# Scaling the exponentials by the reciprocal sums before they are turned, in the second block's attentions, in place of turned reciprocals

## The chip, the cores and the metric

The kernel runs on one NeuronCore of one Trainium2 chip. The metric is the device time of one execution in microseconds (us): 3101.95 us, the median of 3 runs (3101.36 to 3105.1). TensorE (PE in the profile) multiplies and turns tiles; VectorE (DVE), ScalarE (ACT) and GpSimd (POOL) do the elementwise work; SyncE (SP) issues the DMAs. Each engine runs its own list of instructions in order, and semaphores tie the lists together.

## The reference, cut to what matters

Two transformer blocks in float32 on 1024 tokens of width 1024. The first block is not touched. The second has two layers, and each has a memory attention (4 heads of 64, 256 keys); the first layer also has a causal attention of 12 heads. What both compute:

```python
def causal_attention(q, k, v):            # 12 heads; q, k of 96 features, v of 64
    ...                                   # in query blocks of 128 rows
    sc = einsum('bqhd,bkhd->bhqk', q_blk, k) * scale
    sc = where(mask, sc, -inf)
    p = softmax(sc, axis=-1)
    out = einsum('bhqk,bkhd->bqhd', p, v)

def memory_attention_2(q, mem_k, mem_v):  # 4 heads of 64, 256 keys, no mask
    p = softmax(einsum('bshd,bmhd->bhsm', q, mem_k) / sqrt(64), axis=-1)
    return einsum('bhsm,bmhd->bshd', p, mem_v)
...
y = concatenate([tok, mem_out], axis=-1) * silu(gate)
h = layer_norm(ALPHA * h + y @ w_out, ln_g, ln_b)
```

A softmax row is exp(score - maximum) divided by its sum. The division may be done at the end, on the attention's output, or before the product with v, on the exponentials.

## The kernel before, in words

The program is first written as one list, `work`, of records (`emit(kind, r)`); each engine then goes through the whole list and issues its part of every record, with the waits that the record names. So the order in which the Python code emits records is the order on every engine, and nothing is reordered later.

An attention is cut into *units*: one head and one block of 128 queries. Two heads make a *pair*, a first unit (s = 0) and a second one (s = 1, with `mate` set to the first). A unit of the causal attention with query block qt has nblk = qt + 1 key blocks of 128, so its exponentials E are 128 x 128 nblk; a memory unit has nblk = 2. There are 32 memory units in each of the two layers and 96 causal units: 16 + 16 + 48 = 80 pairs. The causal units come as six columns of 16 units (p = 0 to 5), each with nblk = 8, 8, 7, 7, ... 1, 1.

The life of a unit:
- `scores`: TensorE computes the scores in pieces of up to 512 keys; VectorE copies each piece from PSUM into E, scaled (and masked), with the row minimum (L3233, L3238). A causal unit with over 4 blocks has two pieces and a small reduction of the two minima (L3243).
- `exp`: ScalarE takes the exponential of the whole of E in place and sums its rows into `den` (L2998).
- `combine`: for the second unit of a pair, `r_spread`. VectorE waits for both exponentials, takes the reciprocals of the two sums (L3247, 128 x 2) and copies each over 64 columns of a 128 x 128 tile O (L3251).
- `probs`: TensorE turns E in blocks of 128 x 128, up to four into one PSUM place (L2898); ScalarE (L3004) and VectorE (L3269) in turn copy the place into PT.
- `pair_values`: TensorE multiplies PT with v for both heads (L2921), which gives the output with features on the partitions. There the reciprocals are needed along the free axis, so TensorE also turns O (L2924).
- `pair_mul`: VectorE multiplies the gate by the turned reciprocals (L3384) and then by the output (L3386).

`Att.steps` sets the order. Step i emits, in a round: the values of the unit i - 4 if it is the second of its pair (at the start of the step), then in turns a piece of the scores of unit i, a turn of unit i - 2, and the `combine` of unit i - 1; then `pair_mul` and one piece of `fill`, other work of TensorE: gate strips beside the first memory units, projections of the next causal heads beside the causal ones. In the causal attention the exp of unit i comes after its last piece, so on VectorE the order of a step is: first piece of unit i, combine of unit i - 1, second piece of unit i, copy of turned blocks of unit i - 2, reduction. The memory attentions (`together=True`) score the two units of a pair in one even step. E has three buffers in the causal attention (mE), four in the others (gE, nE, lE with one from `cols`); the scores have two PSUM places.

The causal attention lies between 2405 and 2686 us of the span, the memory attention of the first layer at 2282 to 2405 us, that of the second layer at 2830 to 2997 us beside the recurrent branch. There are fewer fills than steps in the causal attention: none runs beside the last 26 units or so, nor beside the last and first few units where column 1 and column 3 begin.

## Time and profile before

| | |
|---|---|
| median of 3 runs | 3101.95 us |
| the profiled execution's own time | 3105.86 us |
| its span | 3104.1 us |
| TensorE busy | 3032.0 us (98%) |
| VectorE busy | 1915.0 us (62%) |
| ScalarE busy | 1373.9 us (44%) |
| GpSimd busy | 717.3 us (23%) |
| TensorE's granted clock over the span | 0.995 of full speed |

The span goes from the first to the last instruction of the profiled execution; the rest of its time lies around it. A busy TensorE is not one at its peak: the end of a matmul is modelled, so the start of one to the start of the next tells what it costs the engine. Idle time of an engine is put down to what came last. A mean over a stage hides that steps of 1 block and of 8 blocks have different limits.

### The profile page before, as it was taken

How to read it: one execution, taken by the hardware profiler on the slowest of the kernel's cores; microseconds unless marked ns; L12 is line 12 of the kernel's file. 1: busy time of each engine (PE TensorE's matmuls, PEld its weight loads, DVE VectorE, ACT ScalarE, POOL GpSimd, SP SyncE). 2: the span in 40 equal slices, each digit the busy share in tenths (PEclk: the TensorE clock that was granted, in tenths of full speed). 3: DMA queues.
4: the chain of work that ended last, by engine and by line, in shares of the span. 5: the costliest groups of instructions: out<-in, count | busy, mean ns of one | idle time of the engine just before them, and what ended most of it. 6: DMA issues, size and time to landing. Idle time of an engine off the chain costs nothing.

```text
span 3104.1 us, 50426 instructions
## 1 busy us (share of the span) xinstructions
PE 3032.0 (98%) x18252; PEld 2572.1 (83%) x18252; DVE 1915.0 (62%) x3747; ACT 1373.9 (44%) x2723; POOL 717.3 (23%) x926
## 2 busy tenths in 40 slices
PE   7999999999999999999999999999999999999999
PEld 7988888999999788888788888888977777687677
DVE  6657675263543655675888887876353657753675
ACT  5446565444444444332333333455433556522552
POOL 3424334366643000001111111001101111022230
PEclk9999999999999999999999999999999999999999
DMA  5110011122211333652233225644100000221012
GB/s 200 43 37 30 21 35 50 31 66 72 72 56 35 138 127 102 227 189 90 72 107 109 106 102 191 210 150 141 51 29 22 16 28 29 96 82 58 28 62 102
DMA packets 96808, 264.84 MB, mean 85 GB/s; under 512 B 19568, under 2 KB 24176, under 8 KB 84144
## 3 DMA queue, kind: packets, MB, share of 16 engines
q1 hardware_dynamic: 96560, 261.61, 24.4%
q8 instruction: 146, 2.39, 0.3%
q14 instruction: 102, 0.84, 0.1%
HBM read 200.69 MB, written 60.62 MB: 84 GB/s over the span
## 4 chain that ended last, share of the span: by engine, by line
PE 85%; DVE 6%; ACT 3%; POOL 2%; issue 2%; DMA 1%; SPq 0%; DVEq 0%; POOLq 0%; ACTq 0%
PE ps L2847 66%; PE ps L2890 7%; PE ps L2898 3%; PE ps L2854 2%; PE ps L2905 2%; PE ps L2921 2%; PE ps L2913 1%; POOL gs L3451 1%; PE ps L2924 1%; PE ps L2941 1%; POOL stats L3459 1%; POOL wlo L3447 1%; DVE qk L3224 0%; DVE hlo L3193 0%; DVE wlo L3116 0%
## 5 line engine op out<-in xcount | busy, mean ns | idle before, releaser
L2847 PE MATMUL ps<-whi,hhi 128*128 128x256 f32 (+2 forms) x1920 | 579.4, 302 | 2.6 <-DVE hlo L3193 1.3
L2847 PE MATMUL ps<-whi,hlo 128*128 128x256 f32 (+2 forms) x1920 | 562.7, 293 | 0.0
L2847 PE MATMUL ps<-wlo,hhi 128*128 128x256 f32 (+2 forms) x1920 | 561.8, 293 | 0.0
L2847 PEld LDWEIGHTS ps<-whi,hhi 128*128 128x128 f32 x1920 | 368.1, 192 | 12.5 <-issue 4.4
L2847 PEld LDWEIGHTS ps<-wlo,hhi 128*128 128x128 f32 x1920 | 368.6, 192 | 7.6 <-issue 0.2
L2847 PEld LDWEIGHTS ps<-whi,hlo 128*128 128x128 f32 x1920 | 368.1, 192 | 7.6
L3456 POOL TENSOR_SCALAR stats<-stats 128x2 f32<-128x2 f32 (+2 forms) x230 | 58.5, 254 | 1142.7 <-ACT xsf L2955 490.0
L3445 POOL CAST whi<-raw 128x512 fp32r<-128x512 f32 (+2 forms) x180 | 113.6, 631 | 832.8 <-PE ps L2847 805.5
L2847 PE MATMUL ps<-hhi,whi 128*128 128x512 f32 x640 | 255.6, 399 | 0.2 <-DVE hlo L3116 0.2
L2847 PE MATMUL ps<-hhi,wlo 128*128 128x512 f32 x640 | 249.9, 390 | 0.0
L2847 PE MATMUL ps<-hlo,whi 128*128 128x512 f32 x640 | 249.2, 389 | 0.0
L3447 POOL TENSOR_TENSOR wlo<-raw,whi 128x512 fp32r<-128x512 f32 (+2 forms) x180 | 230.1, 1278 | 14.4
L3459 POOL TENSOR_TENSOR stats<-stats 128x2 f32<-128x2 f32 (+2 forms) x230 | 167.1, 726 | 19.2
L3451 POOL TENSOR_TENSOR fo<-fo,fo 128x512 f32<-128x512 f32 x44 | 71.3, 1620 | 363.4 <-DVE fo L3346 360.8
L2847 PEld LDWEIGHTS ps<-hhi,wlo 128*128 128x128 f32 x640 | 120.1, 188 | 26.1
L2847 PEld LDWEIGHTS ps<-hhi,whi 128*128 128x128 f32 x640 | 120.4, 188 | 23.8 <-issue 1.3
L2847 PEld LDWEIGHTS ps<-hlo,whi 128*128 128x128 f32 x640 | 120.4, 188 | 23.2
L3224 DVE TENSOR_TENSOR qk<-qk,stats 128x256 f32<-128x256 f32 x148 | 97.6, 660 | 48.8 <-POOL stats L3459 44.9
L3214 DVE COPY qk<-ps 128x256 f32<-128x256 f32 x148 | 62.8, 424 | 94.7 <-PE ps L2847 90.0
L2890 PE MATMUL ps<-mkT,mqT 96*128 96x512 f32 (+3 forms) x288 | 117.6, 493 | 2.1 <-DVE mE L3233 1.6
L3238 DVE CUSTOM_DVE_ANT_1 aE<-ps,atab 128x512 f32<-128x512 f32 x128 | 88.5, 692 | 44.6 <-PE ps L2890 41.2
L2998 ACT ACTIVATE mE<-mE,stats 128x1024 f32<-128x1024 f32 (+7 forms) x96 | 74.5, 776 | 92.6 <-DVE stats L3243 64.1
(783 smaller groups left out, 7443.0 us busy)
## 6 DMA issues: line engine op xcount, KB each, us to landing
raw<-in_W SPq DMA_DIRECT2D x60, 1024.0 KB, 4.9
scratch_fs<-fo SPq DMA_DIRECT2D x77, 256.0 KB, 2.0
scr<-scratch_gates SPq DMA_DIRECT2D x48, 256.0 KB, 3.1
scratch_gates<-go SPq DMA_DIRECT2D x46, 256.0 KB, 2.5
wd<-in_WD SPq DMA_DIRECT2D x44, 256.0 KB, 3.5
wf0b<-in_WF SPq DMA_DIRECT2D x10, 1024.0 KB, 5.1
wf1b<-in_WF SPq DMA_DIRECT2D x10, 1024.0 KB, 5.2
scratch_x<-x SPq DMA_DIRECT2D x16, 512.0 KB, 3.1
```

The costliest lines, as they stand in the source:

```text
L2847: x = e.matmul(r.out, a, b, start=(r.start and m == 0), stop=(r.stop and m == n - 1), skip_group_check=r.joined)
L2854: x = e.transpose(place.ps[0:rows, j * 128:(j + 1) * 128], b, ident[:, :])
L2890: x = e.matmul(p.place.ps[:, o:o + n], *p.blocks[b], start=True, stop=True)
L2898: x = e.transpose(r.place.ps[0:n, j * 128:(j + 1) * 128], r.u.E[:, o:o + n], ident[:, :])
L2998: e.activation(r.e, r.e, ACT.Exp, bias=r.nm, scale=-1.0, accum_out=r.den).then_inc(w.sig(r.done), 1)
L3214: e.tensor_copy(r.nb, r.place.ps[:, 0:256]).then_inc(w.sig(r.place.read), 1)
L3224: e.tensor_tensor(n3, n3, bc, ALU.mult).then_inc(w.sig(r.scaled), 1)
L3238: x = e.tensor_tensor_reduce(out=out, in0=src, in1=p.bias, scale=-u.scale, scalar=3e38, op0=ALU.add, op1=ALU.min, accum_out=p.mx)
L3445: e.tensor_copy(r.hi, r.raw).then_inc(w.inner(), 1)
L3447: e.tensor_tensor(r.lo, r.raw, r.hi.bitcast(F), ALU.subtract).then_inc(w.sig(r.lo_done), 1)
L3451: e.tensor_tensor(r.out, r.a, r.b, r.op).then_inc(w.sig(r.done), 1)
L3459: e.tensor_tensor(r.ss, r.ss, half_neg[:, 0:n], ALU.pow).then_inc(w.sig(r.rstd), 1)
```

## The change

`combine` now emits a record `e_norm` for every unit, not `r_spread` for every pair. VectorE takes the reciprocal of the unit's own sum (128 x 1), and E is multiplied by it in place, before it is turned: by VectorE (`tensor_scalar`), or, for the first unit of each pair of the causal attention (`act_norms=True`), by ScalarE (`Copy` with a scale). The tile O, its copy, its turn on TensorE and the first of the two multiplications of the gate are gone. `probs` waits for the scaled E.

```diff
@@ scored
-                    elif not self.paired:
+                    else:
                         x_.den = stat(1)
-                    elif u.mate:
-                        x_.den = u.mate.den2[:, 1:2]
-                    else:
-                        u.den2 = stat(2)
-                        x_.den = u.den2[:, 0:1]
@@ combine
-                if self.paired and u.mate:
-                    u.oi, u.o, u.O_free = self.O.take()
-                    u.spread = signal("r_spread")
-                    emit("r_spread", u)
+                if self.paired:
+                    u.norm_by_act = self.act_norms and not u.mate
+                    u.inverse = signal("e_norm")
+                    u.normed = signal("exp") if u.norm_by_act else u.inverse
+                    u.ecols = u.E[:, 0:128 * u.nblk]
+                    emit("e_norm", u)
+                    u.e_ready = [u.normed]
@@ attM
-        attM = Att(..., [x[:, :] for x in mO], SB2, OB2, paired=True)
+        attM = Att(..., [], SB2, OB2, paired=True, act_norms=True)
@@ TensorE, pair_value
-                    w.wait_ge(*r.spread)
-                    e.transpose(r.v_place.ps[:, 128:256], r.o, ident[:, :]).then_inc(r.v_place.full[0], 1)
+                    x.then_inc(r.v_place.full[0], 1)
@@ ScalarE
+                elif kind == "e_norm" and r.norm_by_act:
+                    w.wait_ge(*w.last)
+                    w.wait_ge(*r.inverse)
+                    e.activation(r.ecols, r.ecols, ACT.Copy, scale=r.dens[0]).then_inc(w.sig(r.normed), 1)
@@ VectorE
-                elif kind == "r_spread":
-                    w.wait_each(r.mate.exps)
-                    w.wait_each(r.exps)
-                    inner(lambda: e.reciprocal(r.mate.den2, r.mate.den2))
-                    w.wait_ge(*w.last)
-                    w.wait_each(r.O_free)
-                    both = r.mate.den2.rearrange("p (s o) -> p s o", o=1).broadcast_to((128, 2, 64))
-                    e.tensor_copy(r.o.rearrange("p (s d) -> p s d", s=2), both).then_inc(w.sig(r.spread), 1)
+                elif kind == "e_norm":
+                    w.wait_each(r.exps)
+                    w.wait_ge(*w.last)
+                    if r.norm_by_act:
+                        e.reciprocal(r.dens[0], r.dens[0]).then_inc(w.sig(r.inverse), 1)
+                    else:
+                        inner(lambda: e.reciprocal(r.dens[0], r.dens[0]))
+                        w.wait_ge(*w.last)
+                        e.tensor_scalar(r.ecols, r.ecols, r.dens[0], None, ALU.mult).then_inc(w.sig(r.normed), 1)
@@ VectorE, pair_mul
-                    inner(lambda: e.tensor_tensor(r.gate, r.v_place.ps[:, 128:256], r.gate, ALU.mult))
-                    w.wait_ge(*w.last)
                     e.tensor_tensor(r.gate, r.v_place.ps[:, 0:128], r.gate, ALU.mult).then_inc(w.sig(r.v_place.read), 1)
```

On VectorE, the two steps that begin with the first piece of the 7-block units of the last causal column, before. mE is E, mPT is PT, `ISA` is the masked copy of a piece (L3238), gT the gate.

```order
L3233 TENSOR_SCALAR mE_393,stats<-ps 128x512
L3247 RECIPROCAL stats<-stats 128x2
L3251 COPY mO_416<-stats 128x128
L3238 ISA mE_393,stats<-ps,tabM 128x384
L3238 ISA stats 128x1
L3269 COPY mPT_414<-ps 128x512
L3243 TENSOR_REDUCE stats<-stats 128x1
L3233 TENSOR_SCALAR mE_394,stats<-ps 128x512
L3384 TENSOR_TENSOR gT<-ps,gT 128x128
L3386 TENSOR_TENSOR gT<-ps,gT 128x128
L3238 ISA mE_394,stats<-ps,tabM 128x384
```

The same steps on VectorE now (the names of the buffers count otherwise).

```order
L3230 TENSOR_SCALAR mE_394,stats<-ps 128x512
L3247 RECIPROCAL stats<-stats 128x1
L3249 TENSOR_SCALAR mE_393<-mE_393,stats 128x1024
L3235 ISA mE_394,stats<-ps,tabM 128x384
L3235 ISA stats 128x1
L3267 COPY mPT_413<-ps 128x512
L3240 TENSOR_REDUCE stats<-stats 128x1
L3230 TENSOR_SCALAR mE_395,stats<-ps 128x512
L3245 RECIPROCAL stats<-stats 128x1
L3382 TENSOR_TENSOR gT<-ps,gT 128x128
L3235 ISA mE_395,stats<-ps,tabM 128x384
```

In the first of the two steps the copy of 128 x 128 has become a scaling of 128 x 1024; in the second a reciprocal, which waits for the exp of the unit before, stands where the first multiplication of the gate was.

On ScalarE in the same place, before and then now: exponentials (L2998, now L2991), copies of turned blocks (L3004, now L3001), and the new scalings (L2995).

```order
L2998 ACTIVATE mE_393,stats<-mE_393,stats 128x1024
L3004 ACTIVATE mPT_415<-ps 128x512
L2998 ACTIVATE mE_394,stats<-mE_394,stats 128x896
L3004 ACTIVATE mPT_413<-ps 128x512
L2998 ACTIVATE mE_395,stats<-mE_395,stats 128x896
```

```order
L2991 ACTIVATE mE_393,stats<-mE_393,stats 128x1024
L3001 ACTIVATE mPT_413<-ps 128x512
L2991 ACTIVATE mE_394,stats<-mE_394,stats 128x896
L3001 ACTIVATE mPT_411<-ps 128x512
L2995 ACTIVATE mE_394<-mE_394,stats 128x896
L2991 ACTIVATE mE_395,stats<-mE_395,stats 128x896
```

The scaling of a first unit stands between the copy of turned blocks of the unit before it and the exp of its second unit.

## Rows read from the trace of the kernel before

**Rows 1.** The page, busy time, share of the span and instructions of each engine
```profile
PE 3032.0 (98%) x18252; PEld 2572.1 (83%) x18252; DVE 1915.0 (62%) x3747; ACT 1373.9 (44%) x2723; POOL 717.3 (23%) x926
```
**Rows 2.** Busy time by stretch: causal attention; second layer's memory attention
```profile
core 0: us, PE busy (x) PEld busy (x) DVE busy (x) ACT busy (x) POOL busy (x), PEclk, DMA share, GB/s
2405.00:2686.00 281.00, 273.89 (x2016) 200.47 (x2015) 188.56 (x632) 162.32 (x340) 34.38 (x48) 0.99 0.06 21
2830.00:2997.00 167.00, 167.00 (x824) 120.65 (x824) 114.35 (x224) 81.01 (x145) 39.00 (x41) 1.00 0.11 39
```
**Rows 3.** Groups of instructions by line: busy us, mean ns, idle before
```profile
L3386 DVE TENSOR_TENSOR gT<-ps,gT 128x128 f32<-128x128 f32 x80 | 23.3, 291 | 2.7
L3247 DVE RECIPROCAL stats<-stats 128x2 f32<-128x2 f32 x80 | 13.3, 167 | 16.9 <-ACT mE L2998 8.5
L3251 DVE COPY mO<-stats 128x128 f32<-128x128 f32 x52 | 12.7, 244 | 2.0 <-DVE stats L3247 0.2
L2924 PE MATMUL ps<-ident,mO 128*128 128x128 f32 x52 | 17.1, 329 | 0.0
```
**Rows 4.** Timeline of TensorE, causal attention: start us, duration us, instruction
```profile
2657.94 0.61 PE L2921 MATMUL ps<-mPT,mV 128*64 128x128 f32 x8
2658.48 0.33 PE L2924 MATMUL ps<-ident,mO 128*128 128x128 f32 x1
2658.65 1.02 PE L2890 MATMUL ps<-mkT,mqT 96*128 96x512 f32 x2
...
2658.48 0.14 PEld L2924 LDWEIGHTS ps<-ident,mO 128*128 128x128 f32 x1 [0.17 <-issue]
```
**Rows 5.** Timeline of TensorE, first memory attention
```profile
2291.86 0.33 PE L2924 MATMUL ps<-ident,gO 128*128 128x128 f32 x1
2292.03 0.38 PE L2898 MATMUL ps<-ident,gE 128*128 128x128 f32 x2
```
**Rows 6.** VectorE by tile or line: durations of scalings, reciprocals of size and scalar operands
```profile
L3140 DVE TENSOR_SCALAR rt<-rt x2: 227/228/228, 2176.8 to 2178.8; 128x128 f32<-128x128 f32 x2
L3414 DVE TENSOR_SCALAR xc<-up,cols x12: 546/547/993, 2829.2 to 2996.5; 128x512 f32<-128x512 f32 x12
L3206 DVE TENSOR_SCALAR stats<-cols x4: 154/154/156, 87.0 to 87.6; 128x1 f32<-128x1 f32 x4
L3396 DVE TENSOR_SCALAR stats<-stats x16: 213/214/215, 2713.3 to 3097.2; 128x1 f32<-128x1 f32 x16
L3262 DVE SCALAR_TENSOR_TENSOR aE<-aE,stats 128x1024 f32<-128x1024 f32 x32 | 45.0, 1408 | 1.1
```
**Rows 7.** Timeline of ScalarE, last causal column: exponentials of units 81 to 84
```profile
2650.05 1.15 ACT L2998 ACTIVATE mE<-mE,stats 128x1024 f32<-128x1024 f32 x1 [1.48 <-DVE stats L3243]
2653.41 1.04 ACT L2998 ACTIVATE mE<-mE,stats 128x896 f32<-128x896 f32 x1 [1.49 <-DVE stats L3243]
2656.31 1.04 ACT L2998 ACTIVATE mE<-mE,stats 128x896 f32<-128x896 f32 x1 [1.13 <-DVE stats L3243]
2659.31 0.94 ACT L2998 ACTIVATE mE<-mE,stats 128x768 f32<-128x768 f32 x1 [1.23 <-DVE stats L3243]
```
**Rows 8.** Waits of VectorE in the causal attention: us in total, times, longest
```profile
DVE mE L3238 <- PE ps L2890: 47.6, 33, 3.1
...
DVE stats L3247 <- ACT mE L2998: 8.5, 17, 0.7
```
**Rows 9.** Timeline where causal column 1 begins: units 16 and 17
```profile
2461.65 1.15 ACT L2998 ACTIVATE mE<-mE,stats 128x1024 f32<-128x1024 f32 x1 [2.30 <-DVE stats L3243]
...
2463.39 0.60 PE L2898 MATMUL ps<-ident,mE 128*128 128x128 f32 x4
...
2464.37 1.15 ACT L2998 ACTIVATE mE<-mE,stats 128x1024 f32<-128x1024 f32 x1 [1.48 <-DVE stats L3243]
```
**Rows 10.** Timeline at the end of the causal attention: unit 94
```profile
2680.53 0.40 ACT L2998 ACTIVATE mE<-mE,stats 128x128 f32<-128x128 f32 x1 [0.56 <-DVE stats L3238]
...
2681.14 0.14 PEld L2898 LDWEIGHTS ps<-ident,mE 128*128 128x128 f32 x1 [0.20 <-issue]
```
**Rows 11.** Copies of spread reciprocals, second memory attention: ns min/median/max
```profile
L3251 DVE COPY lO<-stats x16: 226/227/1290, 2843.0 to 2979.2; 128x128 f32<-128x128 f32 x16
```

More of the change, by code:

```diff
@@ L654, in build, with __init__ @@
         class Att:
-            def __init__(self, E, PT, os_, sb, ob, dve_turns=True, together=False, paired=False, by_feature=False, between=False):
-                self.by_feature, self.between = by_feature, between
+            def __init__(self, E, PT, os_, sb, ob, dve_turns=True, together=False, paired=False, by_feature=False, between=False, act_norms=False):
+                self.by_feature, self.between, self.act_norms = by_feature, between, act_norms
                 self.E, self.PT, self.O, self.sb, self.ob = Slots(E), Slots(PT), Slots(os_), sb, ob
@@ L764, in pair_values @@
                     self.PT.free[x.pi] = [u.v_place.full]
-                self.O.free[u.oi] = [u.v_place.full]
             def values(self, u):
@@ L2405, in build @@
         gPT = [rest(f"gPT{i}", [256], F, (20 + i) * KB) for i in range(3)]
-        gO = [rest(f"gO{i}", [128], F, 23 * KB + 512 * i) for i in range(2)]
         nE = [inh(f"nE{i}", [256], F, (46 + i) * KB) for i in range(4)]
@@ L2409, in build @@
         mPT = [inh(f"mPT{i}", [T], F, (54 + 4 * i) * KB) for i in range(2)] + [rest("mPT2", [T], F, 80 * KB)]
-        mO = [inh(f"mO{i}", [128], F, 62 * KB + 512 * i) for i in range(2)]
         def post_pair(self, u):
@@ L2438, in build @@
         mem_us = mem_units(kv[0], kv_tok[0], qm_tok)
-        attG = Att([x[:, :] for x in gE], [x[:, :] for x in gPT], [x[:, :] for x in gO], SB2, OB2, together=True, paired=True)
+        attG = Att([x[:, :] for x in gE], [x[:, :] for x in gPT], [], SB2, OB2, together=True, paired=True)
         for s_ in (attG.E, attG.PT, attG.O):
@@ L2447, in build @@
         h_free = [m]
-        attN = Att([x[:, :] for x in nE], [x[:, :] for x in nPT], [x[:, :] for x in mO], SB2, OB2, together=True, paired=True)
+        attN = Att([x[:, :] for x in nE], [x[:, :] for x in nPT], [], SB2, OB2, together=True, paired=True)
         for s_ in (attN.E, attN.PT, attN.O):
@@ L2539, in build @@
         n_done[:] = [mem_us[-1].v_full, mem_us[-1].fin, mem_us[-1].s_full]
-        attM = Att([x[:, :] for x in mE], [x[:, :] for x in mPT], [x[:, :] for x in mO], SB2, OB2, paired=True)
+        attM = Att([x[:, :] for x in mE], [x[:, :] for x in mPT], [], SB2, OB2, paired=True, act_norms=True)
         for s_ in (attM.E, attM.PT, attM.O):
@@ L2696, in build @@
         lPT = [rest(f"lPT{i}", [256], F, o * KB) for i, o in enumerate((71, 87))]
-        lO = [rest(f"lO{i}", [128], F, o) for i, o in enumerate((70 * KB + 512, 88 * KB + 256))]
         attL = Att([x[:, :] for x in lE] + [col("q_norm", 0, 256)], [x[:, :] for x in lPT] + [col("lam"), col("q_norm", 256, 256)],
-                   [x[:, :] for x in lO], SB2, DB_FOUR, together=True, paired=True)
+                   [], SB2, DB_FOUR, together=True, paired=True)
         for s_ in (attL.E, attL.PT, attL.O):
```

## The prediction

> **What bounds the kernel now.** I read the page's busy shares first: TensorE 98% of the span, VectorE 62%, ScalarE 44% [rows 1]. So time is what TensorE spends plus what it waits, and the changed stages have to be looked at one by one. The busy time by stretch shows two sorts. In the second layer's memory attention TensorE is busy for all of its 167 us and VectorE for 114: TensorE alone bounds it. The causal attention has TensorE at 274 of 281 us, VectorE at 189, ScalarE at 162 [rows 2]. There the mean hides something, since the end of a matmul is modelled. VectorE idles 47.6 us before L3238 because scores are late, so mostly TensorE is the late one, but 17 of its reciprocals wait for an exp [rows 8]. The timeline of the exponentials in the last causal column shows the other limit: starts at 2650.05, 2653.41, 2656.31 and 2659.31, each of them ended by a VectorE reduction [rows 7]. That is a loop and not TensorE: exp of unit i - 1, then on VectorE the reciprocal that waits for it, the second piece of unit i, the copy of turned blocks, the reduction, and the exp of unit i. I call a step even or odd by its unit i. Before, only even steps hold the wait for the exp (the reciprocals of a pair are taken once), and they take 3.36 us (81 to 82) where the odd one takes 2.90 us (82 to 83).
>
> **The change part by part.** *TensorE loses 80 turns of O.* In the causal attention the turn starts 0.17 us after a pause that stands ahead of it, and the scores start 0.17 us after the turn [rows 4]. The start-to-start cost is therefore 0.34 us at most, if the pause goes too (it stands ahead of the change from values to a turn, and scores follow now). It is 0.11 us at least, which is the step from one turn to the next (four turns span 0.60 us, two 0.38: 0.22 us for two more) [rows 5, 9]. The pause probably goes and the scores' own weight load, 0.18 us of the 0.36 for two, stays partly in sight; I take 0.25. In the memory attentions turns of E follow instead, 0.17 us later [rows 5]; the pause passes to them, and they take over the slower first turn, so I take 0.12, between 0.11 and 0.17. Gain: 32 pairs x 0.12 = 3.8 us; and 48 causal pairs, of which I leave out the 8 of the last column (bound by the loop), 40 x 0.25 = 10.0 us. Sum 13.8 us, bounds 7.9 (72 x 0.11) and 21.8 (48 x 0.34 + 32 x 0.17).
>
> *VectorE's load.* It loses 80 multiplications of 0.291 us, 80 copies of 0.244 and 80 reciprocals of 0.167 [rows 3], and gains 160 reciprocals, which I price at the same 0.167, as a fixed part makes nearly all of it, and 112 scalings: 64 of 128x256, 48 of 128x128 to 128x1024. The trace has no in-place scaling with one per-row scalar. Bounds: 128 wide without such a scalar 0.228 us, 512 wide with two of them 0.546; the scalar costs 0.06 (0.214 against 0.154 for one column) [rows 6]. So 512 wide without is 0.426, the slope 0.516 ns a column, and with one scalar 0.35 us for 256, 0.68 for 896, 0.75 for 1024. The dear side is the in-place two-input form, 1.41 us for 1024 [rows 6]. I take the cheap side, since its rows are the same operation. In the causal attention that is -33.7 us and +16 + 48 x 0.52 = +41 us: VectorE goes from 189 to some 196 of 281 us, no bound by itself. In the memory attentions the sum is 32 x 0.535 less and 32 x 0.167 + 64 x 0.35 more, +10.6 us, hidden behind TensorE, which is busy throughout [rows 2]; were that cover gone, it would cost those 10.6 us.
>
> The Trainium skill (VectorE: DVE Perf Modes, "The perf-mode tier table") gives `tensor_scalar` on float32 in SBUF two elements a cycle and two-input forms one. Rows 6 agree: 0.516 ns a column is half of the 1.04 ns that a cycle takes at the page's 0.96 GHz. By the two-input rate the sum would be the slower rival's.
>
> *ScalarE's load.* 48 copies with a per-row scale, priced as the exp of the same width, 1.15 us for 1024 down to 0.40 for 128 [rows 7, 10], mean 0.78: +37 us, 162 to 199 of 281. Not a bound, but it stands in the way, below.
>
> *The wait that the change adds.* VectorE now waits in every step for the exp of unit i - 1. Queued behind that waiting reciprocal are the second piece of unit i, the copy of turned blocks that frees TensorE's place, and the reduction on which the exp of unit i waits. Even steps keep their wait, but the 0.23 us copy becomes a scaling of the 8- or 7-block unit: 0.75 - 0.23 = +0.52 us. Odd steps get the loop. I price it from the even step measured: 3.36 us, less 0.11 for the shorter exp (1.04 for 1.15), plus 0.06 for one multiplication of the gate instead of the copy, 3.31 against 2.90: +0.41. A pair of 7-block units takes 0.93 us more. This shows only where the loop and not TensorE sets the pace. Columns 1, 3 and 5 have no fill there, and columns 2 and 4 are about balanced, column 0 half: 5.5 x 0.93 = 5.1 us. The odd step of the 8-block pair in columns 1, 3 and 5, 2.72 us from exp to exp [rows 9], gets about the same 0.4: 1.2 us. In column 5 the 6- and 5-block pairs lose perhaps 0.3 and 0.2: 0.5 us. In columns 2 and 4 a fill's copy, the copy of turned blocks and the scaling queue up on ScalarE in an odd step: 0.3 each, 0.6 us.
>
> *Latency of a first unit.* Its turns need exp, reciprocal, ScalarE's scaling. For unit 16 the first turn starts 0.59 us after the exp ends at 2462.80 [rows 9], for unit 94 the weight load 0.21 us after [rows 10]. What must fit in now is 0.2 for the sum's read, 0.17 and 1.15 us for unit 16, 0.17 and 0.40 for unit 94, so 0.9 and 0.6 us late. For the large ones I count this within the loop; for the last units of the columns I add 1.5 us in all (0 to 3).
>
> Cost: 5.1 + 1.2 + 0.5 + 0.6 + 1.5 = 8.9 us. Net 13.8 - 8.9 = 4.9 us less. Against the profiled execution's own 3105.9 us (span 3104.1) that is 3101.0; that execution was 3.9 us above the median, so against the median I forecast 3097.0 us.
>
> The late side of the shared scaling has a rule against it. The copies of spread reciprocals in the second memory attention take 0.227 us, but one took 1.29 [rows 11]; GpSimd is busy for 39 of those 167 us and 34 of 281 in the causal attention [rows 2]. The Trainium skill (SBUF — State Buffer, "Who interferes with whom") says that such a VectorE form and GpSimd lock each other out of a shared port pair for a whole instruction. By it 12% of 48 scalings would meet GpSimd and wait about 0.5 us, 3 us of VectorE's time, of which a fifth may lie in the loop: 0.6 us more.
>
> **The rivals.** *A, all of it is hidden.* If TensorE has enough ahead (the scores have two places, the turns lag by two steps), the loop's growth is absorbed. For it: 47.6 us of VectorE's idle time is for TensorE [rows 8]. Against: the four exp starts at the pace of the loop [rows 7]. Time: 48 x 0.25 + 3.8 = 15.8 us less, 3086.1.
>
> *B, slower: the scaling on VectorE costs a cycle an element and lies in the loop.* Then it is 1.41 us for 1024 [rows 6], 0.66 more than I took, 0.57, 0.48 and 0.38 more for the next sizes, 2.1 us a column and 12.6 for six; the 6- and 5-block pairs of columns 0 to 4 would fall to the loop as well, 5 x 0.75 = 3.8. Cost 8.9 + 16.4 = 25.3, net +11.5 us: 3113.5. It decides (over +6.2 us net) once the 24 scalings of 5 to 8 blocks take 0.46 us more each than I took, 1.14 us for 896. For it: the in-place form's row. Against: both `tensor_scalar` rows.
>
> *C, the turn frees less than its start-to-start time.* If the pause passes to the next instruction everywhere and a turn is worth 0.11 us, the gain is 7.9 against 8.9 of cost: +1.0, 3103.0. For it: after values the pause is there each time [rows 4], and I know no values followed straight by scores. Against: the scores after the turn start without a pause.
>
> **How the numbers follow.** A measurement of this kernel can tell about 0.2% (6.2 us) from no change: faster is under 3095.8, slower over 3108.2. My forecast, 51%, has a range of its own of 3092 to 3102, with 21% in faster, 29% in the same, 1% in slower. A 20%, faster. C 16%, the same. B 13%, slower. So 41% faster, 45% the same, 14% slower. The range, 3086 to 3107, takes in C and most of A and leaves out B.
>
> **What would show it.** Right: no L2924; TensorE's scores following the last values by about 0.1 us; VectorE's scaling of 128x896 at 0.68 us and ScalarE's at 1.04 to 1.06; exp starts in the last column near 3.9 and 3.3 us apart for the 7-block pair; the stretch of the causal attention 1 to 3 us shorter, columns 0 to 4 giving and the last one taking 3; the memory attentions shorter by 1 to 2 us each. Wrong: a causal attention that is 8 us or more shorter (A), VectorE's scaling of 896 over 1.1 us (B), or a pause of 0.17 us ahead of the scores that follow values (C). A reload of ScalarE's tables between an exp and a scaling would overturn the price of ScalarE's part.

## The result, and the profile after

| | median, us | all runs, us |
|---|---|---|
| before | 3102.64 | 3101.36 to 3105.1 (4) |
| after | 3159.32 | 3157.34 to 3163.96 (4) |

The ratio is 1.0184, 95% interval 1.0166 to 1.0202: the change costs 56.7 us. Forecast were 3097.0 us, with 3086 to 3107 as the range. The profiled execution took 3156.1 us from first to last instruction. Its page has nearly the same TensorE work in a longer span:

```profile
PE 3034.2 (96%) x18172; PEld 2564.1 (81%) x18172; DVE 1935.7 (61%) x3779; ACT 1411.9 (45%) x2771; POOL 719.0 (23%) x926
```

Against [rows 1] the 80 matmuls are gone, and yet TensorE is busy 2.2 us longer and idle 50 us longer. VectorE has gained 20.7 us, ScalarE 38.0. No engine is full. The stretches of [rows 2], after (busy us of each engine, TensorE's granted clock, DMA):

```profile
2405.00:2686.00 281.00, 257.66 (x1834) 183.58 (x1832) 181.86 (x585) 185.63 (x356) 34.40 (x47) 0.99 0.06 20
2830.00:2997.00 167.00, 150.65 (x694) 109.13 (x694) 89.13 (x185) 61.66 (x116) 43.84 (x47) 0.95 0.09 32
```

In the same microseconds less is done: TensorE idles 23 us of 281 where it idled 7, and 16 of 167 where it idled none. In the second stretch its clock is 0.95, not 1.00.

**Where the time went.** There are 16272 matmuls besides the turns, and they come in the same order, with the same operands, in every kernel of this study; only in e7 do 528 of them, all in the first block, change places. So the start of the n-th can be subtracted from its start before. The growth of that difference over a stretch is what the kernel lost there, in one execution of each kernel. Between the causal attention and the second memory attention, and behind it, where the programs are equal, it grows by at most 0.1 us; in an unchanged causal attention by -1.1 to +0.5, so a causal figure is good to about 1 us. (The first block, ahead of all this, differs by 0.3 to 4.3 us from one kernel to the next though its program is the same, e7's apart; the stretches leave it out.) After, in us:

| | first memory attentions | causal attention | second memory attention |
|---|---|---|---|
| predicted | -1 to -2 | -1 to -3 | -1 to -2 |
| after | +2.8 | +25.2 | +27.4 |

The sum is 55.4. The execution was 3.1 us ahead of the one before when the first of them began, by chance. From the first scores of one causal column to those of the next, the 25.2 us are 0.8, 4.1, 1.4, 4.3, 5.9 and, for the last column, 8.7: every column but the first lost more than the noise, not the last one alone.

**The prices of the operations were right, but for one.** Groups by line over the whole second block (busy us, mean ns, idle before); the last line has the least, median and greatest duration in ns:

```profile
L3249 DVE TENSOR_SCALAR mE<-mE,stats 128x1024 f32<-128x1024 f32 x6 | 4.5, 753 | 0.2
L3249 DVE TENSOR_SCALAR mE<-mE,stats 128x896 f32<-128x896 f32 x6 | 4.1, 687 | 0.2
L3247 DVE RECIPROCAL stats<-stats 128x1 f32<-128x1 f32 x112 | 18.4, 164 | 24.9 <-ACT mE L2991 16.0 <-ACT nE L2991 0.3 <-ACT gE L2991 0.3
L2995 ACT ACTIVATE mE<-mE,stats 128x1024 f32<-128x1024 f32 x6 | 6.9, 1149 | 6.8 <-DVE stats L3245 6.8
L2995 ACT ACTIVATE mE<-mE,stats 128x128 f32<-128x128 f32 x6 | 2.4, 401 | 7.7 <-DVE stats L3245 7.7
...
L3249 DVE TENSOR_SCALAR lE<-lE,stats x24: 352/354/1332, 2864.2 to 3030.5; 128x256 f32<-128x256 f32 x24
```

Forecast were 0.75, 0.68, 0.167, 1.15, 0.40 and 0.35 us. The last holds for the median only: 11 of the 32 scalings of the second memory attention were longer, by 5.4 us in all (the last section has why). Most of what was wrong is not in this list: it is in what waits for these instructions. Waits of TensorE and ScalarE in the causal attention, 2405 to 2740 (us in total, times, longest); lines 1 and 2 are TensorE's matmuls and weight loads, and "issue" is time in which the loads waited for nothing that the profile names:

```profile
PE ps L2892 <- ACT mE L2995: 27.2, 28, 1.7
PEld ps L2892 <- issue: 64.5, 115, 2.2
ACT mE L2995 <- DVE stats L3245: 42.5, 24, 3.3
```

Before, the weight loads of the turns of mE had

```profile
PEld ps L2898 <- issue: 28.1, 112, 0.4
```

and TensorE waited there 0.2 us for ScalarE. TensorE now stands at the turns of E (L2892, L2898 before), 28 times and up to 1.7 us, for ScalarE's scaling (L2995); that one stands up to 3.3 us for VectorE's reciprocal (L3245). One such case, the first of the two 3-block units of the last column, from the timeline of all engines (start, duration, idle before and who ended it):

```profile
2693.41 0.62 ACT L2991 ACTIVATE mE<-mE,stats 128x384 f32<-128x384 f32 x1
2693.84 0.30 PEld L2884 LDWEIGHTS ps<-mkT,mqT 96*128 96x128 f32 x2 [0.17 <-issue]
...
2694.89 0.56 DVE L3235 CUSTOM_DVE_ANT_0 mE<-ps,tabM 128x384 f32<-128x384 f32 x1 [1.42 <-PE ps L2884]
...
2695.49 0.69 DVE L3267 COPY mPT<-ps 128x512 f32<-128x512 f32 x1
2696.29 0.16 DVE L3245 RECIPROCAL stats<-stats 128x1 f32<-128x1 f32 x1
...
2696.55 0.61 ACT L2995 ACTIVATE mE<-mE,stats 128x384 f32<-128x384 f32 x1 [2.42 <-DVE stats L3245]
...
2697.19 0.62 ACT L2991 ACTIVATE mE<-mE,stats 128x384 f32<-128x384 f32 x1
...
2697.30 0.52 PE L2892 MATMUL ps<-ident,mE 128*128 128x128 f32 x3 [1.67 <-ACT mE L2995]
```

The exponential is done at 2694.0. The reciprocal of its sum stands on VectorE behind two copies, and the first of them waits 1.42 us for TensorE's scores of the unit that follows. So it comes 2.2 us late, though it needs nothing but the exponential. The scaling follows at once, and TensorE, which takes its work in order, idles 1.67 us at the turn. From the exponential's end to the turn it takes 3.27 us here; the kernel before has 1.65 for this unit, and 0.21 for the 1-block unit of [rows 10], where nothing lies in between. The next exponential is late as well, 3.78 us after the last where the kernel before has 2.35 for this pair.

In the second memory attention TensorE waits for VectorE's own scaling. Waits of TensorE, 2830 to 3060 (before there were none), the longest of them on TensorE, and what VectorE did meanwhile:

```profile
PE ps L2892 <- DVE lE L3249: 16.8, 8, 4.4
PE ps L2892 <- DVE cols L3249: 3.8, 2, 2.3
```

```profile
2892.35 0.70 PE L2884 MATMUL ps<-kv,qm 64*128 64x256 f32 x4
2897.48 0.66 PE L2892 MATMUL ps<-ident,lE 128*128 128x128 f32 x2 [4.43 <-DVE lE L3249]
```

```profile
2889.73 2.29 DVE L3426 TENSOR_TENSOR_SCAN hs<-av,tv 128x1024 f32<-128x1024 f32 x1
2892.05 1.22 DVE L3429 TENSOR_TENSOR gT<-gg,hs 128x1024 f32<-128x1024 f32 x1
2893.31 0.55 DVE L3410 TENSOR_SCALAR xc<-up,cols 128x512 f32<-128x512 f32 x1
2893.89 2.33 DVE L3414 SCALAR_TENSOR_TENSOR xc<-up,cols,xc 128x512 f32<-128x512 f32 x3
2896.26 0.42 DVE L3267 COPY lPT<-ps 128x256 f32<-128x256 f32 x1
2896.78 0.16 DVE L3247 RECIPROCAL stats<-stats 128x1 f32<-128x1 f32 x1
2896.98 0.35 DVE L3249 TENSOR_SCALAR lE<-lE,stats 128x256 f32<-128x256 f32 x1
```

The last two exponentials before this were over at 2882.2. The 0.5 us of reciprocal and scaling stand behind the recurrent branch's scan, product and convolution, which the step before put into VectorE's queue, and TensorE pays for it: 20.6 us in ten places. In six of the ten, the shorter ones, the scaling just ahead of the turn was itself one of the lengthened ones, by 3.9 us together; the rest is the place in the queue.

### The profile page after: what moved, and what is told of

It is laid out like the page before. It is cut to its first block, busy times and chain, and to the rows that moved or that the text cites. A ratio compares the mean times of both kernels' runs of the same rounds, so it can differ in the third digit from the quotient of the medians.

```text
span 3156.1 us, 50474 instructions
## 1 busy us (share of the span) xinstructions
PE 3034.2 (96%) x18172; PEld 2564.1 (81%) x18172; DVE 1935.7 (61%) x3779; ACT 1411.9 (45%) x2771; POOL 719.0 (23%) x926
## 3 DMA queue, kind: packets, MB, share of 16 engines
q1 hardware_dynamic: 96560, 261.61, 23.7%
## 4 chain that ended last, share of the span: by engine, by line
PE 79%; DVE 10%; ACT 4%; issue 2%; POOL 2%; DMA 1%; DVEq 0%; SPq 0%; ACTq 0%; POOLq 0%
PE ps L2841 63%; PE ps L2884 5%; PE ps L2892 3%; PE ps L2899 2%; PE ps L2848 2%; PE ps L2915 2%; PE ps L2907 1%; POOL gs L3447 1%; DVE mPT L3267 1%; POOL stats L3455 1%; POOL wlo L3443 1%; ACT mE L2995 1%; DVE wlo L3113 0%; DVE qk L3221 0%; PE ps L2934 0%
## 5 line engine op out<-in xcount | busy, mean ns | idle before, releaser
L2841 PE MATMUL ps<-whi,hhi 128*128 128x256 f32 (+2 forms) x1920 | 579.2, 302 | 2.3 <-DVE hlo L3190 1.3
L2841 PE MATMUL ps<-whi,hlo 128*128 128x256 f32 (+2 forms) x1920 | 562.1, 293 | 0.0
L2841 PE MATMUL ps<-wlo,hhi 128*128 128x256 f32 (+2 forms) x1920 | 561.9, 293 | 0.0
L2841 PEld LDWEIGHTS ps<-whi,hhi 128*128 128x128 f32 x1920 | 367.8, 192 | 12.5 <-issue 4.3
L2841 PEld LDWEIGHTS ps<-wlo,hhi 128*128 128x128 f32 x1920 | 368.3, 192 | 7.6 <-issue 0.2
L2841 PEld LDWEIGHTS ps<-whi,hlo 128*128 128x128 f32 x1920 | 367.6, 191 | 7.8
L2841 PE MATMUL ps<-hhi,whi 128*128 128x512 f32 x640 | 258.9, 405 | 0.2 <-DVE hlo L3113 0.2
L2841 PE MATMUL ps<-hhi,wlo 128*128 128x512 f32 x640 | 252.6, 395 | 0.0
L2841 PE MATMUL ps<-hlo,whi 128*128 128x512 f32 x640 | 252.2, 394 | 0.0
L2841 PEld LDWEIGHTS ps<-hhi,wlo 128*128 128x128 f32 x640 | 121.8, 190 | 26.6
L2841 PEld LDWEIGHTS ps<-hhi,whi 128*128 128x128 f32 x640 | 122.2, 191 | 25.1 <-issue 1.6
L2841 PEld LDWEIGHTS ps<-hlo,whi 128*128 128x128 f32 x640 | 122.4, 191 | 23.8
L2892 PEld LDWEIGHTS ps<-ident,mE 128*128 128x128 f32 x432 | 52.2, 141 | 77.1 <-issue 64.5
```

What stands on the lines that cost most here:

```text
L2841: x = e.matmul(r.out, a, b, start=(r.start and m == 0), stop=(r.stop and m == n - 1), skip_group_check=r.joined)
L2892: x = e.transpose(r.place.ps[0:n, j * 128:(j + 1) * 128], r.u.E[:, o:o + n], ident[:, :])
```

## The experiments

Each kernel is the one before with both ways in it; a flag `norm` on an attention picks the new one, and then its combine stage has

```
+ if self.paired and self.norm:
+     u.norm_by_act = <first unit of a pair, where act_norms>
+     emit("e_norm", u)          # reciprocal, scaling; the turns wait for it
+     u.e_ready = [u.normed]
  elif self.paired and u.mate:
      ... emit("r_spread", u)    # the way before
```

Two theories were set against each other. *Place*: reciprocal and scaling stand late in an in-order queue, and TensorE stands at the turn. *Load*: the time that the scalings take on the engines binds. (A third, *carry-over*, that the delay of one attention spoils the next, is tested by e1 to e3.) The table holds all results; the three columns on the right are what each lost in a stretch against the kernel before, read as above.

| kernel | median, us | ratio [95%] | first mem. | causal | second mem. |
|---|---|---|---|---|---|
| e1 new way in the causal attention only | 3134.30 | 1.0101 [1.0086, 1.0116] | 0.0 | +29.6 | 0.0 |
| e2 in the second memory attention only | 3130.05 | 1.0089 [1.0073, 1.0106] | 0.0 | +0.5 | +27.8 |
| e3 in the first memory attentions only | 3106.57 | 1.0013 [1.0004, 1.0022] | +2.8 | +0.5 | 0.0 |
| e4 no scaling at all | 3093.11 | 0.9969 [0.9958, 0.9980] | -1.4 | -6.2 | -1.8 |
| e5 VectorE scales everything | 3162.47 | 1.0192 [1.0177, 1.0208] | +2.8 | +29.2 | +27.2 |
| e6 all scalings one column wide | 3138.77 | 1.0112 [1.0097, 1.0127] | +1.6 | +9.6 | +23.1 |
| e7 scaling at the head of the step | 3181.48 | 1.0252 [1.0236, 1.0267] | +0.5 | +29.5 | +23.7 |
| e9 causal, 5 to 8 blocks only | 3116.17 | 1.0040 [1.0026, 1.0054] | 0.0 | +14.1 | 0.0 |
| e10 second mem., scaling right behind exp | 3101.35 | 0.9994 [0.9984, 1.0003] | 0.0 | -1.1 | -1.8 |
| e11 all mem., right behind exp | 3102.47 | 0.9997 [0.9989, 1.0006] | +1.4 | 0.0 | -1.8 |
| e12 causal, ScalarE's scalings one column | 3117.68 | 1.0047 [1.0033, 1.0061] | 0.0 | +14.8 | 0.0 |
| e13 causal, VectorE's one column | 3127.11 | 1.0076 [1.0062, 1.0090] | 0.0 | +23.4 | 0.0 |
| e14 causal, right behind exp | 3147.61 | 1.0141 [1.0126, 1.0156] | 0.0 | +44.7 | 0.0 |
| e15 causal, behind the next exp | 3216.68 | 1.0369 [1.0352, 1.0387] | 0.0 | +109.3 | 0.0 |

**e1, e2, e3: one part each.**

```
e1: attM = Att(..., norm=True, act_norms=True)   # G, N, L as before
e2: attL = Att(..., norm=True)
e3: attG, attN = Att(..., norm=True)
```

> Only the causal attention scales its exponentials; the three memory attentions keep the turned reciprocals. Queue theory (TensorE, in order, stands at the turn of E for a scaling that is queued late on VectorE or ScalarE, and each stage pays by itself): about 25 us slower than before (24.9 minus -0.3 between the same matmuls in the traces of before and after), 3127. Carry-over theory (the causal attention's delay or its lower clock spoils the stages behind it): the whole loss or most of it, 40 us or more.

> Only the memory attention of the second layer (beside the recurrent branch) scales its exponentials. Queue theory: about 27 us slower than before, 3130, with the same idle time of TensorE ahead of turns (20 us) and a granted clock of 0.95 in that stretch. Carry-over theory: under 10 us.

> Only the memory attentions of the first layer scale their exponentials. Queue theory: 2 to 4 us slower (the traces differ by 2.9 us across that stretch), as the fills are short there and the waits small. The prediction's own sum for this stretch was 2 us faster (16 pairs at 0.12 us).

The parts cost 31.8, 27.6 and 4.1 us, 63.5 together against 56.7 for all. So they add up roughly, the loss is no carry from one to the next, and each part is slower by itself. The causal part's 31.8 (29.6 in its stretch) are more than the 25 that the trace led me to expect. Why is not shown; that it starts from another state where the attention ahead of it is the old one is a guess.

**e4: how much there was to win.** It leaves the division out: no turn of O, no copy, no reciprocal, no scaling, and one multiplication of the gate in place of two.

```
- emit("e_norm", u)
- u.e_ready = [u.normed]
```

> Leaves out the division by the row sums in all of the second block's attentions: no reciprocals, no turned tile, no scaling, one multiplication of the gate; the rest is as in the changed kernel. It prices what the removal can give at most. The prediction's gain of 13.8 us (7.9 to 21.8): 3081 to 3095, most likely 3088. If the turns were worth only 0.11 us each: 3094. If the last causal column's loop also gets shorter, up to 5 us more is gained.

It gains 9.4 us, by its time and by the stretches: 32 pairs give 3.2 us, 0.10 each, the 48 causal pairs 6.2 us, 0.13 each (by about 0.02 either way, as the causal figure is good to 1 us). I had 0.12 and 0.25. VectorE's part is gone here too, so 9.4 us is the most that the turns alone can be worth. Where the difference is shows in the waits of the weight loads in the causal attention, before first and then e4 (L2897 is its scores line):

```profile
PEld ps L2924 <- issue: 7.4, 43, 0.2
```

```profile
PEld ps L2897 <- issue: 10.8, 56, 0.3
```

The pause of 0.17 us that stood ahead of the turn of O [rows 4] now stands ahead of the scores, which had 2.5 us of such pauses before: 8.3 us more there, 7.4 gone. The timeline of the changed kernel has it too: 0.17 us ahead of the scores' load at 2693.84. Taking out a turn gives its 0.13 us and no pause.

**e5: no sharing.**

```
- norm_by_act = act_norms and not u.mate
+ norm_by_act = False
```

> As the changed kernel, but VectorE scales all 96 causal units (ScalarE none). Of two theories of the +56.7 us, the first (place: the reciprocal and the scaling stand at the end of a step's work in an in-order queue, and TensorE, in order too, stands at the turn) expects little from the change of engine: the hop from VectorE to ScalarE and ScalarE's longer scaling go (0.40 to 1.15 us become 0.29 to 0.83), but VectorE's queue, which holds the scores copies, grows by 48 scalings, some 25 us; 3150 to 3170 us. The second (load: what binds is the time of the scalings on the engine that carries them) expects VectorE to bind in the causal attention, 182 us of work becoming 207: slower than the changed kernel, 3175 us or more. If sharing was useless, it comes at or below 3155.

3162.5 against 3159.3, inside the range of place: in the causal attention 29.2 us lost instead of 25.2. The share that ScalarE takes saves perhaps 4 us, no more; e1, which has that share, lost 29.6 in the same stretch, so even the 4 are not certain. That VectorE carries 25 us of scalings more and it costs so little speaks against load on VectorE.

**e6: the waits without the durations.** The rest of the exponentials stays unscaled.

```
- u.ecols = u.E[:, 0:128 * u.nblk]
+ u.ecols = u.E[:, 0:1]
```

> As the changed kernel with every reciprocal, every scaling instruction and every wait, but each scaling multiplies one column of its unit's tile instead of all 128 to 1024 (the rest of the exponentials stay unscaled: that division is left out). The place theory expects most of the loss to stay, since the turns still wait for a reciprocal and a scaling at the end of the queue: 3130 to 3150 us, with TensorE still standing at the turns of E. The load theory expects the loss to go with the durations: 3095 to 3112 us.

35.4 us stay of 56.7, and they are not spread evenly: the second memory attention keeps 23.1 of 27 us, the causal one 9.6 of 25 to 30. TensorE's waits at the turns are, causal first,

```profile
PE ps L2908 <- ACT mE L3015: 14.7, 16, 1.5
```

```profile
PE ps L2908 <- DVE lE L3277: 13.3, 6, 4.3
PE ps L2908 <- DVE cols L3277: 3.7, 2, 3.0
```

(L2908 is the turn, L3015 and L3277 are the scalings.) So the second memory attention is mainly a matter of place; the 3.6 us that its waits are short of the 20.6 are nearly the 3.9 of the lengthened scalings, which are not there at one column (0.216 us at most). In the causal one durations matter too.

**e12, e13: whose durations.** Based on e1.

```
e12: u.ecols = u.E[:, 0:1 if u.norm_by_act else 128 * u.nblk]
e13: u.ecols = u.E[:, 0:1 if not u.norm_by_act else 128 * u.nblk]
```

> The new way only in the causal attention (31.8 us when whole), and there ScalarE's scalings, of the first unit of each pair, multiply one column instead of 128 to 1024 (the division of the rest of these units is left out); VectorE's stay whole. Of the 25 us that the causal attention lost in the trace of the changed kernel, about 15 went when all scalings had one column. If ScalarE's part carries them (its scaling stands ahead of the second unit's exponential, so it lengthens the loop): 10 to 13 us less, 3119 to 3124 us. If VectorE's carries them: 0 to 4 us less, 3129 to 3134.

> The mirror of the run before: the new way only in the causal attention, ScalarE's scalings whole, VectorE's, of the second unit of each pair, one column wide (the rest of their division left out). If ScalarE's part carries the loss by durations: 2 to 5 us less than with all whole, 3128 to 3132 us. If VectorE's carries it: 10 us less or more, 3118 to 3124.

Both times lie just below the range that fitted best, 3119 to 3124 and 3128 to 3132. Of e1's 29.6 us in the stretch 14.8 go with ScalarE's durations and 6.2 with VectorE's, 21 together. e6, with both, is 20 below e1, but only 15.6 below the changed kernel on which it is built: they add, to some 5 us. So in this attention both theories have a share: the durations cost 16 to 20 us, and place and waits without them 15.8 (e6's 9.6 and the 6.2 of gain that e4 has and e6 has not). But ScalarE's durations do not act as I wrote. The exponentials of the first pair of the last column start 3.26 us apart in e12, and 3.26 us apart after; VectorE sets that step either way. What falls is the time from the end of a first unit's exponential to its turn: for the 8 blocks of the last column 2.16 us in the changed kernel, 1.31 in e12, 0.59 before.

**e7: earlier, in all attentions.**

```
- ((self.scores, scored), (self.probs, [unit(i - lag_t)]), (self.combine, [unit(i - 1)]))
+ ((self.combine, [unit(i - 1)]), (self.scores, scored), (self.probs, [unit(i - lag_t)]))
```

> As the changed kernel, but in each step of the second block's attentions the reciprocal and the scaling of the unit before stand at the head of the step, ahead of the next unit's scores copies and of the copies of turned blocks; nothing is left out. The place theory expects the turns to wait less: in the second memory attention 10 to 20 us of TensorE's 27 come back, in the causal one the short units gain, while VectorE's reciprocal, now waiting for the exponential ahead of the next scores copy, lengthens the loop of the 8- and 7-block units by up to 1 us a unit (12 to 24 us over six columns): 3135 to 3160 us. The load theory expects the same time as the changed kernel, 3155 to 3163, since no duration changes.

The edit reached further than I meant: the tuple orders the first block's attentions too, and it was already 23.7 us behind when the second block's first attention began. So its total, outside both ranges, tells nothing of the place. By stretches, the second memory attention lost 23.7 in place of 27.4, far from the 10 to 20 us expected back; the causal one lost as much as e1. The head of the next step is still behind the recurrent branch's work, which belongs to the end of this one: ahead of TensorE's longest wait there (5.5 us) VectorE's reciprocal follows the same scan, product and convolution.

**e9: long units only.**

```
- if self.paired and self.norm:
+ if self.paired and self.norm and u.nblk > 4:
```

> The kernel before, with the new way only in the causal attention and there only for the units of 5 to 8 key blocks (48 of 96); the units of 1 to 4 blocks and the memory attentions stay as before. With all causal units the new way cost 31.8 us. The place theory (short units have nothing between a unit's exponential and its turn, and TensorE stands there) expects a small part of it: plus 5 to 12 us, 3108 to 3115. The load theory, by which the columns scaled decide (624 of 864 blocks are in these units, 72%), expects 72% of it: plus 23 us, 3125.

12.8 us, a little over what place gave and well under load's 23. The long units have 72% of the columns and less than half of the loss (14.1 of 29.6 us). So the columns scaled do not set the loss by themselves.

**e10, e11: right behind the exponential.** The emission moves from the combine stage of the next step to the end of the scores stage.

```
  for u in us:
      u.e_ready = list(u.exps)
+     if self.norm:
+         emit("e_norm", u)
+         u.e_ready = [u.normed]
```

> The kernel before, with the new way only in the second memory attention, where with the changed kernel's order it cost 27.6 us. Here the reciprocal and the scaling of a unit stand right behind its exponential in the program, ahead of the recurrent branch's work of the same step (scan, convolution, gates), instead of behind it. The place theory: VectorE reaches them one or two microseconds after the exponential, long before TensorE comes to the turn, and TensorE's waits at the turns of lE (16.8 us, longest 4.4) go to under 3; what stays is that VectorE waits for ScalarE's exponentials in between, 12 times about 1 us on an engine that is busy about half of the stretch; 3098 to 3110 us. The load theory, since durations and counts stay: 3125 to 3132.

> As the run just before, and the first memory attentions too (the new way with the reciprocal and the scaling right behind the exponential); the causal attention as before. It is the candidate for a kernel that beats the one before: 32 turns of spread reciprocals go, worth 0.12 us each, 3.8 us. If the place was all that was wrong in the memory attentions: 3097 to 3104 us. If the waits of VectorE for the exponentials cost the recurrent and the gate chains: 3104 to 3115.

In e10 the whole loss of the second memory attention is gone: -1.8 us, exactly e4's gain. VectorE's queue now reads so (L3276 reciprocal, L3278 scaling; the exponentials of this pair end at 2882.13 and 2882.76):

```profile
2882.25 0.16 DVE L3276 RECIPROCAL stats<-stats 128x1 f32<-128x1 f32 x1 [0.50 <-ACT lE L3012]
2882.45 0.63 DVE L3278 TENSOR_SCALAR lE<-lE,stats 128x256 f32<-128x256 f32 x1
2883.18 0.16 DVE L3276 RECIPROCAL stats<-stats 128x1 f32<-128x1 f32 x1
2883.38 0.35 DVE L3278 TENSOR_SCALAR lE<-lE,stats 128x256 f32<-128x256 f32 x1
```

No wait of TensorE for a scaling is left in the stretch. Of VectorE, the wait for the exponentials is small, and the stretch has TensorE full again at full clock:

```profile
DVE stats L3276 <- ACT lE L3012: 10.3, 16, 1.5
```

```profile
2830.00:2997.00 167.00, 167.00 (x816) 120.45 (x816) 121.87 (x241) 82.88 (x147) 38.58 (x40) 1.00 0.10 37
```

VectorE works 7.5 us more here than before (121.87 against 114.35) and it costs nothing: load is refuted for this stretch. In the first memory attentions the same placement only halves the loss, to +1.4, where e4 gained 1.4; what keeps it there was not looked into. Neither kernel beats the one before by what can be measured: e10 is the best of the kernels that still divide by the sums, and its interval reaches from 0.9984 to 1.0003.

**e14, e15: the causal attention, as early and as late as can be.** e14 has e10's edit, for the causal attention alone. In e15 the step's tuple leaves out combine, and at the step's end there stands

```
+ if self.norm and unit(i - 1):
+     drain(self.combine(unit(i - 1)))
```

> The new way only in the causal attention (31.8 us when whole), with the reciprocal and the scaling of a unit right behind its exponential in the program, ahead of the next unit's scores copies: what cured the second memory attention. If the place is what is wrong here too: 3108 to 3118 us. If the loop is (VectorE now waits out each exponential before it may copy the next scores, so exponential, reciprocal, copy, maximum and the next exponential stand in one ring): 3128 to 3140, no better than with the changed kernel's order; the run that put the scaling at the head of the step lost 29 us in this stretch.

> The new way only in the causal attention, with the reciprocal and the scaling of a unit behind the next unit's exponential, at the very end of the step: ScalarE's scaling no longer delays that exponential (its durations cost 16.6 us of the 31.8), but the unit's turn comes later. If the ring of exponentials is what binds: 3110 to 3122 us. If TensorE, which stands at the turn, binds: 3130 to 3150.

Both are worse than e1, by 13.3 and 82.4 us, and outside every range that I had given: I had the direction of e14 (no better than e1) and nothing of e15. The waits of e14, then of e15 (L2909 and L2910 are the turns, L2901 and L2902 the scores, L3012 and L3013 the exponentials, L3017 ScalarE's scaling):

```profile
ACT mE L3012 <- DVE stats L3261: 69.8, 43, 3.2
DVE stats L3274 <- ACT mE L3012: 50.2, 48, 1.5
DVE stats L3276 <- ACT mE L3012: 35.8, 30, 1.6
```

```profile
DVE mE L3257 <- PE ps L2902: 114.1, 59, 4.2
PEld ps L2910 <- issue: 107.6, 102, 3.8
PE ps L2910 <- ACT mE L3017: 60.1, 38, 3.0
```

In e14 VectorE waits 86 us for exponentials ahead of its reciprocals and ScalarE 70 us for the reductions behind them: a ring. In e15 no scaling stands ahead of the next exponential; TensorE waits at the turn instead, and VectorE 114 us for the scores that TensorE would compute behind it. The order of the changed kernel lies between the two and is, with e7's, the best of the four; in this attention the loss is there at every place tried. So no run cures it, and that the place is the cause here is shown only for the part that e6 keeps without durations.

## Why the prediction was wrong

- *"Hidden behind TensorE, which is busy throughout" (memory attentions)*: this is the step that failed there, and the largest miss: 27.4 us in the second one for a cost set at nothing, and 2.8 in the first ones. I weighed 10.6 us of VectorE's time against TensorE's and forgot that the scaling is a link to TensorE's turn. Before, what TensorE needed late was only the copy of O, one per pair and not before the values. The turns waited for the exponential itself, on ScalarE. Now they wait for VectorE's queue, with six instructions of the recurrent branch in it. e10, with the same work at another place, loses nothing.
- *The latency of a first unit, 1.5 us in all, "for the large ones counted within the loop"*: this is the step that failed in the causal attention. I counted 0.2, the reciprocal and the scaling, as if the reciprocal ran when the exponential ended. It stands behind a scores copy that waits for TensorE. The turn of the 8-block unit of [rows 9] begins 2.16 us after the exponential instead of 0.59, 1.57 late where I had 0.9; for the 3-block unit above it is 3.27 instead of 1.65. In all I had 8.9 us of cost for this attention; measured are 25.2 lost and the 6.2 of gain (e4) not had, 31.4.
- *The loop*: sizes nearly right where I looked. Steps of the 7-block pair of the last column (starts 2667.00, 2671.12, 2674.38, 2677.78 against [rows 7]):

```profile
2667.00 1.15 ACT L2991 ACTIVATE mE<-mE,stats 128x1024 f32<-128x1024 f32 x1
...
2671.12 1.04 ACT L2991 ACTIVATE mE<-mE,stats 128x896 f32<-128x896 f32 x1 [2.25 <-DVE stats L3240]
...
2674.38 1.04 ACT L2991 ACTIVATE mE<-mE,stats 128x896 f32<-128x896 f32 x1 [0.43 <-DVE stats L3240]
...
2677.78 0.94 ACT L2991 ACTIVATE mE<-mE,stats 128x768 f32<-128x768 f32 x1 [1.63 <-DVE stats L3240]
```

  4.12 and 3.26 us, forecast 3.9 and 3.3. But I took the loop for a matter of the 8- to 5-block units. In the last column the exponentials from first to last take 41.2 us instead of 34.2: 2.6 us more in the first seven steps, down to the second 5-block unit, and 4.5 in the eight behind it, where the step from a first unit to its second grew by 1.1 to 1.7 us. For those I had 1.5 us in all six columns. And columns 0 to 4, which were to give, lost 16.5 us together.
- *13.8 us from 80 turns*: measured 9.4 (e4). In the memory attentions 0.10 in place of 0.12, in the causal one 0.13 in place of 0.25, since the pause moves on to the scores. That is rival C's mechanism, and its sum of 7.9 was the nearest; its time, 3103.0, rests on the same 8.9 us of cost and failed with it. The gain that was missing, 4.4 us, would by itself have left the result in the stated range.
- *Rival B* had the right sign by the wrong mechanism: its condition, scalings at one element a cycle, is refuted by 687 ns for 896 columns, and with it its time, 3113.5. *Rival A* (all hidden) is refuted by the causal attention's 25.2 us. ScalarE's tables are not reloaded between exponential and scaling: no table load lies in the causal attention, before or after.
- *Waiting out GpSimd, 3 us of VectorE's time, 0.6 us beside the sum*: in the causal attention it was under 0.4 us in all. It came where it was not counted, in the second memory attention: 5.4 us of VectorE's time and 3.9 of TensorE's waits.
- *VectorE's load in the causal attention, "no bound by itself"*: right, as far as e5 shows. Durations do count there, for 21 us of the 35.8 that e1's loss and the gain not had make together, and most of it ScalarE's. That they count on the way from an exponential to its turn is what e12's times suggest; it was not tested apart.
- *What neither term had*: TensorE's clock. Windows around the 4.43 us pause above, and at the end of the causal attention:

```profile
2880.00:2893.00 13.00, 12.90 (x64) 9.93 (x64) 8.57 (x12) 7.57 (x11) 0.00 (x0) 1.00 0.24 82
2893.00:2897.50 4.50, 0.07 (x3) 0.05 (x1) 4.15 (x9) 0.05 (x1) 0.00 (x0) 0.78 0.00 0
2897.50:2903.00 5.50, 5.50 (x16) 4.40 (x17) 4.35 (x11) 2.22 (x4) 0.00 (x0) 0.56 0.00 1
2700.00:2705.00 5.00, 1.88 (x19) 1.31 (x18) 3.04 (x14) 2.42 (x8) 0.00 (x0) 0.94 0.00 0
2705.00:2710.00 5.00, 4.04 (x18) 2.59 (x19) 3.21 (x8) 3.04 (x7) 0.00 (x0) 0.50 0.15 39
```

  After the pause TensorE works without a gap at a granted clock of 0.56. The 128x512 matmuls of L2841 there (2830 to 3040) take 416, 405 and 404 ns on average; their like before took 400, 390 and 389, and e10's take 400, 390 and 390. 584 of them times 15 ns make some 9 us: with the 20.6 of pauses and less the 1.8 of gain about 28, near the 27.4 measured. The clock's own rows say the same: in this attention it stood at 0.50 in four pieces (2895.5 to 2902.3, 2936.5 to 2939.9, 2974.0 to 2980.9, 3015.0 to 3018.4), where TensorE was busy for 16.8 us, of which half, 8.4, would not have been needed at full clock. The split is worked out, not tested: no run has the pauses without the slower clock.

What stays open: how the causal attention's 9.6 us without durations divide between the reciprocal's place and the hop to ScalarE; why e1 lost 4 us more there than the changed kernel; what keeps the first memory attentions from gaining; and whether turns one step later, with a fourth tile for E, would hide the causal loss. That was not tried.

## What to carry to other kernels

When a value gains one more operation on its way to TensorE, do not ask only whether the engine has time for it, but what stands ahead of it in that engine's queue when TensorE comes; cover by a busy TensorE means nothing for an instruction that TensorE waits for. Emit such an operation right behind what feeds it, unless this closes a ring with the next unit's input, as in e14. And read the gain of a removed instruction with its pause passed on to its successor, until a run shows the pause gone.

## What the runs showed of the hardware

A scaling on VectorE that takes 0.354 us in the median took up to 1.33 us after, and up to 1.42 in e10. VectorE and GpSimd, in e10:

```profile
2877.59 1.42 DVE L3278 TENSOR_SCALAR lE<-lE,stats 128x256 f32<-128x256 f32 x1
```

```profile
2877.59 1.27 POOL L3475 TENSOR_TENSOR wlo<-raw,whi 128x512 fp32r<-128x512 f32 x1
```

Both start together, and the scaling ends 0.15 us after GpSimd's 1.27 us: it has waited out the other instruction. After, the 1.33 us scaling starts at 2878.62, 0.08 us into a 1.26 us instruction of GpSimd, and ends 0.15 us behind it. It is no single case: in the second memory attention 11 of 32 scalings last over 0.5 us after, 9 of 32 in e10, 5.4 us too long together in either, and each of the twenty ends 0.15 us after an instruction of GpSimd (a cast or a `tensor_tensor`). The rule of the Trainium skill that the prediction used (SBUF — State Buffer, "Who interferes with whom") says just that, and the trace agrees; in e10 it happened in a queue with slack and cost nothing, while after it made up 3.9 of the 20.6 us that TensorE waited.

The other is the clock. A TensorE that idles for 4.43 us is granted 0.56 for the next 5.5 us, and at the end of the causal attention, where it was busy 1.88 us of 5, 0.50 for the 5 us behind (1.2 of 2.4 GHz). A shorter pause can do it: 2.32 us up to 2935.83 were followed by 0.50 from 2936.5 to 2939.9, all of it work without a gap. But not each pause does: the clock fell four times for ten pauses. So here the pauses cost more than their length: for the ten of the second memory attention some 9 us on 20.6, by the estimate above.
